# Second feed-forward layer with seven block products for eight in its up projections

## Chip, cores and metric

One core of one Trainium2 chip runs the whole kernel. The metric is the device time of one execution in microseconds. The kernel before takes 2902.94 us (median of 3 runs, 2902.27 to 2908.03).

## What is computed

The reference is a trunk of two layers on 1024 tokens of width 1024, with 16 meta tokens prepended: a neighbourhood attention, a grouped-query attention, and a feed-forward layer behind each. Only the second feed-forward layer is touched by the change:

```python
def rmsnorm(x, g):
    y = x32 * lax.rsqrt(jnp.mean(x32 * x32, axis=-1, keepdims=True) + RMS_EPS)
    return y.astype(x.dtype) * g

def swiglu(h, w1, w3, w2):
    return (jax.nn.silu(h @ w1) * (h @ w3)) @ w2

h = h + swiglu(rmsnorm(h, norm_ffn[i]), ffn_w1[i], ffn_w3[i], ffn_w2[i])
```

`h` has 1024 tokens here (the meta tokens are dropped after the attention of this layer), w1 and w3 are 1024 x 2816, w2 is 2816 x 1024, all float32.

## The kernel before

Everything is kept transposed: features on the 128 partitions, tokens along the free axis. The residual stream `h` is [128, 8, 1044], eight chunks of features. A float32 product is made of three passes in `fp32r`: each operand is split into a high part (rounded by writing it as `fp32r`) and a low part (what is left), and TensorE adds high x high, high x low and low x high. `uh` and `ul` hold the two parts of the input of the layer (`h` times its gain); the factor 1/rms of a token (`rstd`) is applied behind the product.

Weights come through two slots. SP loads a raw block into `wraw` (`fetch`, L384), GpSimd writes `wh` (L506, a multiplication by one) and `wl` (L509, the difference) and counts up `s_wrd`; TensorE multiplies the unit and counts up `s_un`, which frees the slot for GpSimd. A `unit` of the up projections (L695) is four feature chunks x three passes x two PSUM groups of 512 tokens, 24 matmuls with one weight block of 128 x 512; two units make a `dense`, one output block of 128 hidden columns.

`ffn(l)` works in rounds of 256 hidden columns, eleven of them (`FIT`). A round has four `dense` of the up projections (w1 and w3, for two output blocks b) in two sets of PSUM banks, and the down projections of the round before: eight units of 12 matmuls with weight blocks of 128 x 256. VectorE takes w1's product times rstd (L1571), ScalarE applies silu (L1212), VectorE multiplies by rstd (L1574) and by w3's product (L1577), ScalarE makes the high part of the gated row (L1214) and VectorE its low part (L1579). The down products are added to `h` by VectorE (L1559). The loops are written out per engine in the same order and are held together by counting semaphores: `s_wrd`, `s_un`, `s_df` (a PSUM group was read), `s_silu`, `s_sr`, `s_gh`, `s_gr`.

Ahead of the layer stands the output projection of the attention. Its adds to `h` feed squares (L1518 sums them), the parts `uh` and `ul` (L1197, L1522), and at its end `stat` (L729) and `rsqrt` with `refine` (L1528 to L1536), which leave `rstd`. Behind the layer stand the final norm and the stores. Steps of other stages which the rows below show are: the first projections (L1646 makes `ul`), the per-head norm of the attention (L1807, L1862), and its sum of probabilities on GpSimd (L648).

## Time and profile before

| | |
|---|---|
| median of the runs | 2902.94 us |
| profiled execution | 2904.71 us, span 2902.9 us |
| PE (matmul) busy | 2795.3 us, 96% |
| PEld (weight load) busy | 2293.9 us, 79% |
| VectorE (DVE) busy | 1264.5 us, 44% |
| ScalarE (ACT) busy | 663.5 us, 23% |
| GpSimd (POOL) busy | 1381.4 us, 48% |
| granted TensorE clock, mean | 0.986 |

The page gives for each engine the time in which it had an instruction in work, over the span of one execution. Matmuls overlap in the array, so their mean duration is longer than the distance between two starts. The chain that ended last goes back from the last instruction to what released it; a wait shows which engine's semaphore ended it. Over the whole span, 85% of that chain is PE.

### The profile page before, as it was taken

The page shows a single profiled execution, that of the slowest core. Times are in us where ns is not written, and L with a number is a line of the kernel's source. Part 1 is how long each engine was busy: PE and PEld are TensorE (multiplying, and loading weights), DVE is VectorE, ACT ScalarE, POOL GpSimd, SP SyncE. Part 2 cuts the span into 40 slices and gives each one's busy share as a digit, 9 for nine tenths or more (in the row PEclk, how much of TensorE's full clock was granted, in tenths as well). Part 3 has the DMA queues.
Part 4 walks back from the last instruction along what each step waited for, and adds up shares of the span by engine and source line. Part 5 has one row for each costly group of instructions (what it writes and reads, how often), then busy time and mean ns, then how long its engine had stood idle before and what let it go on. Part 6 is the DMA issues. An engine that isn't in the chain of part 4 may idle for free.

```text
span 2902.9 us, 39911 instructions
## 1 busy us (share of the span) xinstructions
PE 2795.3 (96%) x15103; PEld 2293.9 (79%) x15103; DVE 1264.5 (44%) x1644; ACT 663.5 (23%) x1132; POOL 1381.4 (48%) x1399
## 2 busy tenths in 40 slices
PE   6999999899999999999999999998799999999998
PEld 5888888699999999999776444443678888888886
DVE  4454444443322232222878766665352322322225
ACT  3333343311000000000332545543210000000003
POOL 3565555454444444444544745644354444444442
PEclk8999999999999999999999999999899999999999
DMA  8222121511111111111432000000311111111112
GB/s 201 58 72 61 58 66 47 199 44 46 44 47 46 44 46 46 46 47 46 136 70 55 8 15 1 15 15 16 145 44 44 51 51 47 47 47 47 45 45 84
DMA packets 227572, 166.17 MB, mean 57 GB/s; under 512 B 25000, under 2 KB 209744, under 8 KB 227296
## 3 DMA queue, kind: packets, MB, share of 16 engines
q1 hardware_dynamic: 215376, 135.69, 16.6%
q10 hardware_dynamic: 12048, 28.37, 2.7%
q8 instruction: 109, 1.79, 0.3%
q14 instruction: 39, 0.32, 0.0%
HBM read 133.19 MB, written 26.03 MB: 55 GB/s over the span
## 4 chain that ended last, share of the span: by engine, by line
PE 85%; DVE 8%; issue 3%; DMA 2%; ACT 1%; SPq 0%; ACTq 0%; POOL 0%; DVEq 0%; POOLq 0%
PE PS L695 60%; PE PS L822 8%; PE PS L1086 3%; DVE nmx L1900 3%; PE PS L873 2%; PE PS L1100 2%; PE PS L909 2%; PE PS L849 2%; DVE rcp L1929 2%; PE PS L1026 1%; DMA wraw<-in_a_w_qkv 1%; DVE accd L1916 1%; PE PS L887 1%; DVE ssq L1518 1%; PE PS L1044 1%
## 5 line engine op out<-in xcount | busy, mean ns | idle before, releaser
L506 POOL TENSOR_TENSOR wh<-wraw,ones 128x512 fp32r<-128x512 f32 (+1 forms) x456 | 426.7, 936 | 1174.1 <-PE PS L695 1010.2
L509 POOL TENSOR_TENSOR wl<-wraw,wh 128x512 fp32r<-128x512 f32 (+1 forms) x456 | 528.0, 1158 | 35.7
L695 PE MATMUL PS<-uh,wh 128*128 128x348 f32 (+1 forms) x1696 | 451.6, 361 | 18.9 <-DVE q L1670 7.5
L695 PE MATMUL PS<-uh,wl 128*128 128x348 f32 (+1 forms) x1696 | 445.8, 358 | 0.0
L695 PE MATMUL PS<-ul,wh 128*128 128x348 f32 (+1 forms) x1696 | 445.7, 358 | 0.0
L1559 DVE TENSOR_TENSOR h<-PS,h 128x1044 f32<-128x1044 f32 (+1 forms) x192 | 236.9, 1234 | 331.2 <-PE PS L695 316.6
L695 PEld LDWEIGHTS PS<-uh,wh 128*128 128x128 f32 x1696 | 302.1, 189 | 73.9 <-issue 22.5
L695 PEld LDWEIGHTS PS<-ul,wh 128*128 128x128 f32 x1696 | 304.3, 189 | 36.3
L695 PEld LDWEIGHTS PS<-uh,wl 128*128 128x128 f32 x1696 | 303.8, 189 | 36.2
L1212 ACT ACTIVATE at<-at 128x1044 f32<-128x1044 f32 (+1 forms) x44 | 47.1, 1070 | 862.9 <-DVE at L1571 862.9
L695 PE MATMUL PS<-yh,wh 128*128 128x348 f32 x1056 | 226.1, 323 | 5.3 <-DVE h L1559 2.9
L695 PE MATMUL PS<-yl,wh 128*128 128x348 f32 x1056 | 225.0, 321 | 0.0
L695 PE MATMUL PS<-yh,wl 128*128 128x348 f32 x1056 | 224.7, 321 | 0.0
L1571 DVE TENSOR_TENSOR at<-PS,rstd 128x1044 f32<-128x1044 f32 (+1 forms) x44 | 54.4, 1235 | 367.7 <-PE PS L695 367.7
L1900 DVE TENSOR_REDUCE nmx<-PS 128x1 fp32r<-128x1044 f32 x128 | 158.3, 1240 | 123.8 <-PE PS L1026 123.7
L1450 ACT ACTIVATE pf<-PS 128x512 f32<-128x512 f32 (+1 forms) x288 | 170.6, 595 | 180.1 <-PE PS L1086 178.8
L1577 DVE TENSOR_TENSOR at<-PS,at 128x1044 f32<-128x1044 f32 (+1 forms) x44 | 54.4, 1236 | 320.6 <-PE PS L695 320.5
L695 PEld LDWEIGHTS PS<-yh,wh 128*128 128x128 f32 x1056 | 177.8, 188 | 6.6 <-issue 6.4
L695 PEld LDWEIGHTS PS<-yl,wh 128*128 128x128 f32 x1056 | 178.7, 188 | 0.0
L695 PEld LDWEIGHTS PS<-yh,wl 128*128 128x128 f32 x1056 | 177.4, 188 | 0.0
L648 POOL TENSOR_TENSOR accp<-accp,pf 128x1024 f32<-128x1024 f32 x64 | 152.5, 2382 | 28.0 <-ACT pf L1450 25.0
L1100 PE MATMUL PS<-pf,vg 128*64 128x512 f32 x576 | 155.1, 617 | 0.0
(236 smaller groups left out, 3999.1 us busy)
## 6 DMA issues: line engine op xcount, KB each, us to landing
wraw<-in_ffn_w SPq DMA_DIRECT2D x176, 256.0 KB, 2.9
wraw<-in_ffn_w SPq DMA_DIRECT2D x176, 128.0 KB, 2.2
wraw<-in_a_w_qkv SPq DMA_DIRECT2D x48, 256.0 KB, 2.9
biasb<-bias_rows SPq DMA_DIRECT2D x128, 72.0 KB, 2.6
h<-h_spill ACTq DMA_DIRECT2D x16, 522.0 KB, 9.1
h_spill<-h SPq DMA_DIRECT2D x8, 522.0 KB, 8.8
h_spill<-h ACTq DMA_DIRECT2D x8, 522.0 KB, 3.3
xt<-in_x SPq DMA_DIRECT2D x8, 512.0 KB, 10.8
```

Source lines behind the costliest of these rows:

```text
L506: nc.gpsimd.tensor_tensor(wh[:, slot, 0:w], wraw[:, slot, 0:w], ones[:, 0:1].to_broadcast([P, w]), ALU.mult).then_inc(s_whi, 1)
L509: nc.gpsimd.tensor_tensor(wl[:, slot, 0:w], wraw[:, slot, 0:w], wh[:, slot, 0:w].bitcast(F32), ALU.subtract).then_inc(s_wrd, 1)
L648: nc.gpsimd.tensor_tensor(accp[:, :, :], accp[:, :, :], pf[:, (first + kt) % PB, :, :], ALU.add).then_inc(s_pacc, 1)
L695: mm = nc.tensor.matmul(PS[:, set_ + c, 0:cw], w, x[k][:, c * cw:(c + 1) * cw], start=(first and i == 0 and ti == 0), stop=(last and i == ...
L822: mm = nc.tensor.matmul(PS[:, D0 + bk, 0:CW], w, x[c][:, bk * CW:(bk + 1) * CW], start=(c == 0 and ti == 0), stop=(c == 7 and ti == 2), sk ...
L849: mm = nc.tensor.matmul(PS[:, 6 + hd, 0:SN], q, k[:, 5 * x:5 * x + WR + 1, K0[j]:K0[j] + WC], start=True, stop=True)
L873: mm = nc.tensor.transpose(PS[:, 3 + hd, P * c:P * c + P], pb[:, n % 4, a:a + P], ident[:, :])
L1086: mm = nc.tensor.matmul(PS[:, 6 + e, :], k[:, P * kt:P * kt + P], q[:, q0:q0 + QB], start=(i == 0), stop=(i == 1))
L1100: nc.tensor.matmul(PS[64 * e:64 * e + 64, OB[n % 2], :], vg[par][:, kt, :], pf[:, s % PB, e, :], start=(kt == 0), stop=(kt == KT - 1), ski ...
L1450: nc.scalar.activation(pf[q, s % PB, e, :], PS[q, 6 + e, :], ACT.Exp).then_inc(s_gex, 1)
L1559: nc.vector.tensor_tensor(hm, PS[:, set_:set_ + nb, 0:cw], hm, ALU.add).then_inc(s_df, 1)
L1900: nc.vector.tensor_reduce(nmx[:, i:i + 1], PS[:, set_:set_ + 3, 0:CW], AX.XY, ALU.max, negate=True).then_inc(s_mr, 1)
```

## The change

Rounds 2 to 11 of the layer compute their up projections by block products. With the 1024 features, the 256 hidden columns and the 1024 tokens each cut in two, a quad (w1 or w3 of one round) is a 2 x 2 block matrix product of eight blocks; it is made of seven products (Strassen's scheme in Winograd's form), each of 12 matmuls into one PSUM bank, with sums of weight blocks as one operand and sums of blocks of u as the other.

- GpSimd makes four sums of weight blocks for each quad (`sum_of`) and, as before, the high and low parts of each of the seven weight operands (`lo`), all 512 wide, in three slots (`wh3`, `wl3`) from six raw buffers (`rb`). The down projections take four weight loads of 512 a round in place of eight of 256.
- The four sums of u blocks are made once, in round 1: ScalarE writes `h` times gain in 16 copies of 512, VectorE makes four sums and four low parts of 2048, ScalarE four high parts (`block_hi`, `block_lo`). Round 1 itself stays as four `dense`, with its second output block first.
- ScalarE copies the first product of a quad (`snap`); VectorE adds the products up into blocks (`sums`, `gate_quad`, `gated_quad`) and then scales, gates and splits the rows.
- The order on TensorE is: w1's quad of the next round, the down projections of the last one, w3's quad of the next round. The last iteration has both quads and then two sets of down projections.
- Buffers are laid out anew (`ghs`, `ghl`, `tsh`, `tsl`, `bsum`, `upraw` and others).

```diff
+ROLES = [[(0, 1, 2, 3, 4), (1, 4, 2, 5, 3)], [(0, 1, 2, 3, 4), (5, 0, 2, 4, 1)]]
+QBANK = [(0, 1, 2, 7), (5, 3, 6, 4)]
...
+            def fetch_products():
...
+                sp.wait_ge(s_wrd, U_S)
+                sp.wait_ge(s_tl, 3)
+                first(U_S, 1)
+                down(DOWN[0][0], U_S, 0, 0)
+                with sp.Fori(0, ITS - 1) as i:
+                    rest(OPS * i + U_S, i)
+                    first(OPS * i + (U_S + OPS), i + 2)
+                    down(DOWN[0][0], OPS * i + (U_S + OPS), i + 1, 0)
...
-            fetch_ffn(1)
+            fetch_products()
...
+            def split_products():
+
+                def sum_of(dst, x, y, op, c):
+                    nc.gpsimd.tensor_tensor(rb[dst], rb[x], rb[y], op).then_inc(s_wsum, 1)
+                    po.wait_ge(s_wsum, c)
+
+                def lo(o, c, r, load=None):
+                    if load is not None:
+                        po.wait_ge(s_xr[r], load)
+                    po.wait_ge(s_un, U_S + c + (o - 3))
+                    nc.gpsimd.tensor_tensor(wh3[(o + 1) % 3], rb[r], ones[:, 0:1].to_broadcast([P, 512]),
+                                            ALU.mult).then_inc(s_xhi, 1)
+                    po.wait_ge(s_xhi, c + o)
+                    nc.gpsimd.tensor_tensor(wl3[(o + 1) % 3], rb[r], wh3[(o + 1) % 3].bitcast(F32),
+                                            ALU.subtract).then_inc(s_wrd, 1)
+
+                def quad(o, c, s, r, l22, l11, l21, l12):
+                    lo(o, c, r[A22], l22)
+                    lo(o + 1, c, r[A11], l11)
+                    po.wait_ge(s_xr[r[A21]], l21)
+                    sum_of(r[S3], r[A11], r[A21], ALU.subtract, s + 1)
+                    sum_of(r[A21], r[A21], r[A22], ALU.add, s + 2)
+                    sum_of(r[A11], r[A21], r[A11], ALU.subtract, s + 3)
+                    lo(o + 2, c, r[A11])
+                    lo(o + 3, c, r[A21])
+                    lo(o + 4, c, r[S3])
+                    lo(o + 5, c, r[A12], l12)
+                    po.wait_ge(s_wrd, U_S + c + o + 5)
+                    sum_of(r[A12], r[A12], r[A11], ALU.subtract, s + 4)
+                    lo(o + 6, c, r[A12])
...
-            split_ffn(1)
+            for q in range(4):
+                split_pair(U_FF[1] + 2 * q, U_FF[1] // 2 + q)
+            split_products()
...
+            def ffn_of_products():
+                ub, gb = U_FF[1], G_FF[1]
+
+                dense_of_new_u(ub, 3, gb - 2, 1, 5)
+                dense(ub + 2, D1, uhc, ulc, gb, 1)
+                dense(ub + 4, 5, uhc, ulc, gb + 1, 1)
+                pe.wait_ge(s_gm, 1)
+                dense(ub + 6, D1, uhc, ulc, gb + 1, 1)
+
+                def product(n, o, j, bank, first):
+                    pe.wait_ge(s_wrd, n + o)
+                    (xh, xl), a, b = operands[j], wh3[(o + 1) % 3], wl3[(o + 1) % 3]
+                    for k in range(4):
+                        for ti, (w, x) in enumerate(((a, xh), (a, xl), (b, xh))):
+                            mm = nc.tensor.matmul(PS[:, bank, :], w[:, P * k:P * k + P], x[:, k, :],
+                                                  start=(first and k == 0 and ti == 0),
+                                                  stop=(k == 3 and ti == 2), skip_group_check=True)
+                    mm.then_inc(s_un, 1)
+
+                def quad(n, o, t, banks_, adds=None):
+                    a, b, c, d = banks_
+                    if adds is not None:
+                        pe.wait_ge(s_ha, adds + 7)
+                    product(n, o, 0, d, True)
+                    if adds is not None:
+                        pe.wait_ge(s_ha, adds + 8)
+                    product(n, o + 1, 1, a, True)
+                    product(n, o + 2, 2, b, True)
+                    product(n, o + 3, 3, c, True)
+                    pe.wait_ge(s_u2, t)
+                    product(n, o + 4, 4, b, False)
+                    pe.wait_ge(s_snap, t)
+                    product(n, o + 5, 5, a, False)
+                    pe.wait_ge(s_c22, t)
+                    product(n, o + 6, 6, c, False)
...
+                pe.wait_ge(s_tl, 4)
+                with pe.Fori(0, ITS) as i:
+                    n = OPS * i + U_S
+                    pe.wait_ge(s_silu, 2 * i + (K1 + 2))
+                    quad(n, 1, 2 * i + 1, QBANK[0])
+                    pe.wait_ge(s_gr, 2 * i + (K1 + 2))
+                    for d in range(4):
+                        down(n, 8 + d, d, 0, (3, 5), loop_sets(i))
+                    quad(n, 12, 2 * i + 2, QBANK[1], 8 * i)
...
+                def sums(n, o, t, banks_):
+                    a, b, c, d = banks_
+                    dve.wait_ge(s_un, n + (o + 2))
+                    dve.wait_ge(s_snap, t)
+                    tt(u2, PS[:, b, :], s1, ALU.add, s_u2)
+                    dve.wait_ge(s_un, n + (o + 4))
+                    tt(u3[:, :], PS[:, b, :], s1, ALU.add, s_u3)
+                    dve.wait_ge(s_u3, t)
+
+                def gate_quad(n, o, t):
+                    a, b, c, d = QBANK[0]
+                    sums(n, o, t, QBANK[0])
+                    tt(at1[:, 1, right], PS[:, c, :], u3[:, :], ALU.add, s_c22)
+                    tt(at1[:, 1, left], u3[:, :], PS[:, d, :], ALU.subtract, s_c21)
+                    dve.wait_ge(s_c22, t)
+                    dve.wait_ge(s_c21, t)
+                    tt(at1[:, 1, :], at1[:, 1, :], r1, ALU.mult, s_ar)
+                    dve.wait_ge(s_un, n + (o + 5))
+                    tt(at1[:, 0, left], PS[:, a, :], r1[:, left], ALU.mult, s_c11)
+                    dve.wait_ge(s_un, n + (o + 6))
+                    dve.wait_ge(s_u2, t)
+                    tt(at1[:, 0, right], PS[:, c, :], u2, ALU.add, s_c12)
+                    dve.wait_ge(s_c12, t)
+                    tt(at1[:, 0, right], at1[:, 0, right], r1[:, right], ALU.mult, s_ar)
+
+                def gated_quad(n, o, t):
+                    a, b, c, d = QBANK[1]
+                    sums(n, o, t, QBANK[1])
+                    tt(c22[:, :], PS[:, c, :], u3[:, :], ALU.add, s_c22)
+                    tt(u3[:, :], u3[:, :], PS[:, d, :], ALU.subtract, s_c21)
+                    dve.wait_ge(s_c22, t)
+                    tt(at1[:, 1, right], at1[:, 1, right], c22[:, :], ALU.mult, s_b22)
+                    dve.wait_ge(s_c21, t)
+                    tt(at1[:, 1, left], at1[:, 1, left], u3[:, :], ALU.mult, s_gm)
+                    dve.wait_ge(s_un, n + (o + 5))
+                    tt(at1[:, 0, left], at1[:, 0, left], PS[:, a, :], ALU.mult, s_c11)
+                    dve.wait_ge(s_un, n + (o + 6))
+                    dve.wait_ge(s_u2, t)
+                    tt(u2, PS[:, c, :], u2, ALU.add, s_c12)
+                    dve.wait_ge(s_c12, t)
+                    tt(at1[:, 0, right], at1[:, 0, right], u2, ALU.mult, s_gm)
...
+                dve.wait_ge(s_un, ub + 2)
+                taken(1, 5)
+                dve.wait_ge(s_hgt, 2 * KC)
+                tt(b11, b12, b11, ALU.subtract, s_tt)
...
+                gate_row(1, 1)
+                dve.wait_ge(s_un, ub + 4)
+                gated(1, 1, D1)
+                for j, i in enumerate((0, 1, 3)):
+                    block_lo(i, j + 1)
+                dve.wait_ge(s_un, ub + 6)
+                taken(0, 5)
+                gate_row(0, 2)
+                block_lo(2, 4)
+                dve.wait_ge(s_un, ub + 8)
+                gated(0, 2, D1)
+                with dve.Fori(0, ITS) as i:
+                    n = OPS * i + U_S
+                    g_lo(1, 2 * i + 1, 0)
+                    g_lo(0, 2 * i + 2, 0)
+                    gate_quad(n, 1, 2 * i + 1)
+                    gate_row(1, 2 * i + 3)
+                    down(0, 3, *unit_sem(n, 8, 4 * i, 0), s_ha)
+                    gate_row(0, 2 * i + 4)
+                    for m in range(1, KC):
+                        down(m, 5 if m % 2 else 3, *unit_sem(n, 8, 4 * i, m), s_ha)
+                    dve.wait_ge(s_sr, 2 * i + (K1 + 4))
+                    gated_quad(n, 12, 2 * i + 2)
```

`OPS` is 18 and `ITS` 9 (rounds 2 to 10 in a loop, round 11 behind it). `tt` is VectorE's two-operand op, `r1` is `rstd`. `g_lo` makes the low part of a gated row, `gate_row` multiplies a row by `rstd`, both 1024 wide and from SBUF. `s_tl` counts the low parts of the u sums, `s_gm` gated rows, `s_ha` down products added to `h`.

## Rows read from the trace of the kernel before

**Rows 1.** The chain that ended last: start us, us, what.

```profile
2150.96 726.50 PE PS L695 x3144
```

**Rows 2.** Busy time of each engine in a stretch of the second feed-forward layer.

```profile
core 0: us, PE busy (x) PEld busy (x) DVE busy (x) ACT busy (x) POOL busy (x), PEclk, DMA share, GB/s
2200.00:2300.00 100.00, 100.00 (x435) 81.18 (x434) 27.03 (x22) 7.43 (x7) 43.20 (x44) 1.00 0.16 45
```

**Rows 3.** Groups by line and form, 2200 to 2800 us: count, busy us, mean ns, idle before.

```profile
L695 PEld LDWEIGHTS PS<-ul,wh 128*128 128x128 f32 x578 | 108.6, 188 | 25.1
```

**Rows 4.** GpSimd in order of time: start us, us, what, [idle before].

```profile
2467.28 1.04 POOL L506 TENSOR_TENSOR wh<-wraw,ones 128x512 fp32r<-128x512 f32 x1 [3.12 <-PE PS L695]
2468.40 1.30 POOL L509 TENSOR_TENSOR wl<-wraw,wh 128x512 fp32r<-128x512 f32 x1
```

**Rows 5.** All engines in order of time, 26 to 30 us.

```profile
27.09 2.15 POOL L509 TENSOR_TENSOR wl<-wraw,wh 128x512 fp32r<-128x512 f32 x1
29.20 2.04 POOL L506 TENSOR_TENSOR wh<-wraw,ones 128x512 fp32r<-128x512 f32 x1
...
29.49 0.92 PE L695 MATMUL PS<-uh,wh 128*128 128x348 f32 x2 [5.60 <-POOL wl L509]
```

**Rows 6.** Groups by line and form, whole run, as in rows 3.

```profile
L648 POOL TENSOR_TENSOR accp<-accp,pf 128x1024 f32<-128x1024 f32 x64 | 152.5, 2382 | 28.0 <-ACT pf L1450 25.0
...
L1862 DVE TENSOR_TENSOR qc<-qc,PS 128x512 f32<-128x512 f32 x4 | 2.7, 682 | 4.8 <-PE PS L971 4.8
```

**Rows 7.** All engines in order of time, 2400 to 2403 us.

```profile
2400.45 0.63 PE L695 MATMUL PS<-uh,wh 128*128 128x512 f32 x2
2400.65 1.23 DVE L1571 TENSOR_TENSOR at<-PS,rstd 128x1024 f32<-128x1024 f32 x1 [9.95 <-PE PS L695]
...
2400.76 1.04 POOL L506 TENSOR_TENSOR wh<-wraw,ones 128x512 fp32r<-128x512 f32 x1 [3.15 <-PE PS L695]
```

**Rows 8.** All engines in order of time, 2162 to 2170 us.

```profile
2163.91 2.20 DVE L1536 TENSOR_TENSOR rstd<-ssq,oraw 128x1024 f32<-128x1024 f32 x1
...
2166.14 1.23 DVE L1571 TENSOR_TENSOR at<-PS,rstd 128x1024 f32<-128x1024 f32 x1
...
2168.49 1.28 DVE L1574 TENSOR_TENSOR at<-at,rstd 128x1024 f32<-128x1024 f32 x1 [1.13 <-ACT at L1212]
...
2168.78 2.16 POOL L509 TENSOR_TENSOR wl<-wraw,wh 128x512 fp32r<-128x512 f32 x1
```

**Rows 9.** All engines in order of time, 1548 to 1552 us.

```profile
1548.90 1.09 DVE L1807 SCALAR_TENSOR_TENSOR ssq<-ssq,y_gq 96x512 f32<-96x512 f32 x1
...
1549.52 1.62 POOL L509 TENSOR_TENSOR wl<-wraw,wh 128x512 fp32r<-128x512 f32 x1
```

**Rows 10.** The page: a group of part 5, and part 6 (KB, us to landing).

```profile
L1450 ACT ACTIVATE pf<-PS 128x512 f32<-128x512 f32 (+1 forms) x288 | 170.6, 595 | 180.1 <-PE PS L1086 178.8
...
wraw<-in_ffn_w SPq DMA_DIRECT2D x176, 256.0 KB, 2.9
```

**Rows 11.** TensorE in order of time, behind two of its idle times.

```profile
573.13 0.74 PE L695 MATMUL PS<-uh,wh 128*128 128x348 f32 x3 [2.89 <-DVE h L1559]
...
574.24 1.07 PE L695 MATMUL PS<-uh,wl 128*128 128x348 f32 x3
...
577.64 0.64 PE L695 MATMUL PS<-uh,wh 128*128 128x348 f32 x3
...
2058.36 1.05 PE L695 MATMUL PS<-ol,wh 128*128 128x512 f32 x2
2059.22 1.05 PE L695 MATMUL PS<-oh,wl 128*128 128x512 f32 x2
```

**Rows 12.** Busy time and granted clock (PEclk) behind idle times, columns as in rows 2.

```profile
573.00:577.00 4.00, 3.87 (x16) 3.87 (x17) 3.24 (x4) 3.89 (x4) 0.68 (x1) 0.64 0.22 66
1107.00:1112.00 5.00, 3.61 (x23) 3.62 (x24) 1.16 (x1) 0.00 (x0) 2.28 (x2) 1.00 0.39 108
2057.00:2061.00 4.00, 3.65 (x9) 2.88 (x10) 0.21 (x1) 0.00 (x0) 0.00 (x0) 0.50 0.10 28
```

More of the change, by code:

```diff
@@ L91 @@
 ARR, EW = 23, 48
+OPS = 18
+SUMS = 8
+RAWS = 6
+A22, A11, A21, A12, S3 = range(5)
+ROLES = [[(0, 1, 2, 3, 4), (1, 4, 2, 5, 3)], [(0, 1, 2, 3, 4), (5, 0, 2, 4, 1)]]
+DOWN = [(5, 2, 4, 0), (3, 5, 2, 1)]
+TAIL = (0, 4, 3, 5)
+QBANK = [(0, 1, 2, 7), (5, 3, 6, 4)]
 def banks(ap, l=0):
@@ L290, in build @@
         G_WO, G_FF = [25, G_GQ], [34, G_GQ + 9]
-        G_ST = [0, 33, 166, G_FF[1] - 1, G_FF[1] + 132]
+        G_ST = [0, 33, 166, G_FF[1] - 1, G_FF[1] + 10]
+        U_S, ITS = U_FF[1] + 8, FIT - 2
+        U_L = U_S + OPS * ITS
+        K1 = 2 * FIT
         def kview(ap):
@@ L367, in build @@
         s_sum = sem("gqa_sums_done")
+        s_hgt = sem("u_of_ffn1_made")
+        s_tt = sem("u_block_sum_made")
+        s_tbh = sem("u_block_sum_hi_made")
+        s_tl = sem("u_block_sum_ready")
+        s_xr = [sem(f"up_raw{i}_loaded") for i in range(RAWS)]
+        s_wsum = sem("weight_block_sum_made")
+        s_xhi = sem("product_weight_hi_made")
+        s_snap = sem("first_product_copied")
+        s_u2 = sem("two_products_added")
+        s_u3 = sem("three_products_added")
+        s_c22 = sem("block22_made")
+        s_c21 = sem("block21_made")
+        s_c12 = sem("block12_made")
+        s_c11 = sem("block11_read")
+        s_b22 = sem("gated_block22_made")
+        s_ar = sem("gate_row_scaled")
+        s_gm = sem("gated_row_made")
+        s_dn = sem("down_unit_multiplied")
+        s_ha = sem("down_unit_added")
         block = es.enter_context(nc.Block())
@@ L717, in dense_of_new_u @@
                 xh, xl = chunks(u_hi[k]), chunks(u_lo[k])
-                unit(n, 0, D0, xh, xl, range(0, 4), True, False, l, KC * k)
+                unit(n, 0, set_, xh, xl, range(0, 4), True, False, l, KC * k)
                 if k:
@@ L722, in dense_of_new_u @@
                     spread_first()
-                unit(n + 1, 1, D0, xh, xl, range(4, 8), False, True, l, KC * k)
+                unit(n + 1, 1, set_, xh, xl, range(4, 8), False, True, l, KC * k)
             def spread(set_, w, x, l=0):
@@ L763, in down @@
                     pe.wait_ge(s_gr, k)
-                    xh, xl = [gh[l][par][:, b, :] for b in range(2)], [gl[l][par][:, b, :] for b in range(2)]
+                    xh, xl = [gh[par][:, b, :] for b in range(2)], [gl[par][:, b, :] for b in range(2)]
                     for m in range(KC):
@@ L1160, in _ @@
             proj_out(1)
-            ffn(1)
+            ffn_of_products()
             pe.wait_ge(s_ssq, 4)
-            pe.wait_ge(s_df, G_FF[1] + 132)
+            pe.wait_ge(s_df, G_FF[1] + 10)
             for i in range(8):
```

257 lines of the change are left out of this document (236 added, 21 removed).

## Prediction

> **What bounds the kernel now.** I read the chain of work that ended last first. From 2150.96 us it is one piece of 726.50 us, 3144 matmuls of `unit` (L695), and it ends 25 us before the span does [rows 1]. That piece is the second feed-forward layer but for its first 24 matmuls, so this layer is TensorE's: 0.2311 us a matmul of 512 columns (726.50 / 3144), 5.55 us for a unit of 24, 66.5 us for a round of 288. Busy time by stretch says the same: PE 100 of 100 us at full clock, GpSimd 43, VectorE 27 [rows 2]. TensorE is the only engine whose removed work is worth time here, and GpSimd has about half of each round free. The question is what GpSimd and VectorE do to each other once GpSimd is filled.
>
> **The change, part by part.** A round is the up projections of 256 hidden columns, in two quads A (w1) and B (w3), and the down projections D of the round before. Round 1 stays dense.
>
> *Matmuls.* A quad takes 7 products of 12 matmuls for 96: 12 fewer, twice a round, ten rounds: 240 x 0.2311 = **-55.5 us**. A product takes 2.77 us, a quad 19.4, D 22.2, a round 61.0. I keep 0.2311: each matmul has a weight load of its own already, 188 ns, beside a matmul of 231 [rows 3].
>
> *GpSimd's work.* A weight block costs 1.04 + 0.08 + 1.30 us [rows 4]; the next op starts 0.04 before the last ends (27.09 + 2.15 against 29.20) [rows 5]: 2.38 us a block. A sum of two blocks is a two-input op of 512: 1.30, as `wl`, and 0.08 for its own semaphore. The 1024-wide sum took 2382 ns [rows 6], so half of it, 1.19, is the lower bound; 1.40 is my upper. Down weights are now loaded 512 wide, four of 2.38 for eight smaller pairs. A quad is 7 x 2.38 + 4 x 1.38 = 22.2 us of GpSimd for 19.4 of TensorE; D is 9.5 for 22.2. The round's sum, 53.9, fits under 61.0, but the order is A, D, B, A, D, B: B and A follow each other, 44.4 us against 38.8, and with three weight slots GpSimd enters them only two blocks ahead. That is a local deficit whatever the averages say.
>
> *VectorE against GpSimd.* Here the trace speaks against the change. GpSimd's op of 1.04 is still 1.04 beside a VectorE op that reads PSUM (L1571, all of it overlapped) [rows 7]. Beside a VectorE op that reads two SBUF tensors, one waits for the other: `wl` at 2168.78 took 2.16 for 1.30, behind L1574; and the other way round L1536, started while a `wl` was in work, took 2.20 for 1.23 [rows 8]. So an op of 1024 costs GpSimd 2.16 - 1.30 = 0.86 us. For 512 wide: `wl` at 1549.52 took 1.62 beside L1807, that is 0.32 lost [rows 9]. The change adds such ops while GpSimd has no slack: `gate_quad` and `gated_quad` scale and multiply in SBUF (one of 1024 and four of 512 a round), and the two `g_lo` of 1024 now fall on the start of A. Ops on PSUM (`u2`, `u3`, blocks 22, 21, 12, the adds to `h`) cost GpSimd nothing. The Trainium skill ("SBUF — State Buffer", Who interferes with whom) states that a VectorE instruction with two SBUF inputs and a GpSimd one that reads SBUF exclude each other for the whole instruction. The row agrees with who is blocked, not quite with how long; by whole instructions (1.23 and 0.68) the stall below would be 1.8 us longer in each of nine rounds, 16 us more in all.
>
> *The stall in a round.* I follow GpSimd from the end of D. Blocks B1 and B2 are ready and B's three sums end 1.2 us later. Until A3 is ready come 8 blocks, 19.0, and 4 sums, 5.5; three VectorE ops of 512, 1.0; two `g_lo`, 1.7; waits for slots, 0.3 (a slot is free 0.31 after the next unit starts, 2400.76 against 2400.45 [rows 7]). Ready at 28.7 to 29.0. TensorE gets to A3 after nine products, 25.0. It restarts 0.25 after `wl` (27.09 + 2.15 to 29.49 [rows 5]): **4.25 us idle at A3**. From A4 on a product is longer than a block, so GpSimd keeps up but for the fourth sum and the `ar` op of 1024: 0.6 us at the first D. Nine times 4.85 = 43.7 us. The last round has no D between its quads: GpSimd needs 22.2 + 3 us of losses for B's 19.4, 5.5 idle, and some 1 in the downs: 6.5.
>
> *Start.* rstd is ready at 2166.1 and VectorE takes the first row then [rows 8]. New behind that on its queue: four block sums of 2048 (an estimate of 2 x 1.23 - 0.15 = 2.3 each), excluded by GpSimd's splits in turn (3.4 lost, and 0.9 for TensorE on a late split), before `gated(1)`, which now ends at 2183. The fourth dense of round 1 waits for it (`s_gm`), due at 2179: 4.0 late. Then three low parts, a row, silu, the last high part (which waits for unit 7) and low part: 2197, where TensorE is done at about 2194: 3.2. GpSimd's first blocks wait for loads that SP holds until `s_tl` 3: 1.15 at A1 and 5.2 at A3. Together 13.5.
>
> Other edits I cost at nothing. The loads: the closest one (A11 of B) is issued three units before its use, over 5 us, and a 256 KB load lands in 2.9 [rows 10]. PSUM reads: `u2`, `u3` and block 22 take 0.68 each [rows 6] and have a product of 2.77 to do it in. ScalarE's 16 copies of 512 for the block sums, 0.6 each [rows 10], are 9.6 us beside VectorE's rsqrt chain and over before it. The tail after the last add is unchanged.
>
> Sum so far: -55.5 + 43.7 + 6.5 + 13.5 = **+8.2 us**.
>
> *The clock.* What a stall does next decides the size. Behind 2.89 us without a matmul the granted clock was 0.64 in 573 to 577; behind the long wait that ends at 2057 it was 0.50 until 2061: the lower of the two levels, 1.2 GHz for 2.4, at which matmuls of 512 start 0.43 apart [rows 11, 12]. The 5 us from 1107, with 1.4 idle, kept 1.00 [rows 12]. There will be eleven stalls of over 4 us. A low stretch of about 3.4 us (574.2 to 577.6 in rows 11) costs 8 x (0.43 - 0.231) = 1.6; 0.5 of that is taken from the stall at D; 1.1 x 11 = **+12 us**. Bounds: nothing, and twice that stretch (the long wait had at least 4 us), 30.
>
> Total +20 us. The profiled execution took 2904.71, with a span of 2902.9, 1.8 above the median of the runs; the difference applies to either: **2923 us**.
>
> **The rivals.**
> 1. *The exclusion costs nothing* (VectorE's ops fall into gaps of GpSimd). The stall at A3 is then 28.9 - 2.7 + 0.25 - 25.0 = 1.5; that at D goes, the start costs 6 and the last quad 3: 22 in all, no stall long enough for the clock. -55.5 + 22 = -33: **2869**. For it: averages leave room. Against it: GpSimd has no gaps between B and A, and rows 8 and 9 show the loss whenever two such ops meet. It decides from the point where stalls in a round, clock included, are under 3.9 us (55.5 less 20 for start and end, over nine).
> 2. *The port costs as above, but the clock stays up*: +8: **2911**. For it: a gap of 1.4 us did nothing; against it both longer ones.
> 3. *The clock stays low twice as long*: +8 + 30: **2941**.
> 4. *Half-way*: sums of 1.19 (4 x 0.11) and half of the meetings avoided (1.4) take 1.8 off each stall at A3, which is then 2.4 and mostly too short for the clock: 8.2 - 9 x 1.8 - 4 at start and end, -12: **2891**.
> That the change does not do what it says, TensorE paying per product what it saves, I give 2 in 100: nothing in rows 3 hints at it.
>
> **How the numbers follow.** Forecast 0.45; rival 1 0.15; 2 0.17 (half of its spread inside 0.2%); 3 0.12; 4 0.09; the last 0.02. This measurement can tell about 0.2%, 5.8 us, from no change. Faster: 0.15 + 0.09 = 0.24. Same: 0.12. Slower: 0.64. The forecast's own range is 2910 to 2942; the range for 8 in 10 reaches down towards rival 1 and over rival 3: 2878 to 2946.
>
> **What would show it.** In the profile after: about 240 fewer matmuls; a round near 66.9 us against 66.5; PE at some 91% in this layer, with ten idle times of over 4 us at the third product of A, ended by GpSimd's `wl`; GpSimd near 90%, its ops of 1.04 and 1.30 at 1.4 to 2.2 where `g_lo` or `ar` meets them; VectorE's `g_lo` at 2.0 to 2.3 for 1.23; a granted clock of 0.95 to 0.97 there. It is wrong if GpSimd's mean op stays at 1.04 and 1.30, if idle at A3 is under 3 us, or if another engine ends the wait (VectorE through `s_c22` or `s_ha`, a load).

## The result, and the profile after

The changed kernel takes 2926.01 us (median of 4 runs, 2923.73 to 2930.06) against 2904.65 for the kernel before (4 runs, 2902.27 to 2908.03): ratio 1.0074, 95% interval 1.0056 to 1.0092. It is slower by 21 us, where 2923.0 was forecast. The profiled execution has a span of 2921.9 us at a mean granted clock of 0.975 (before 2902.9 and 0.986).

In the lines of after, L920 issues the matmuls of the block products, L954 those of the down projections, L852 the dense ones; GpSimd makes sums at L646, high parts at L653, low parts at L656; nearly all of VectorE's work is L1917, so there one goes by tiles (`gls` is written by `g_lo`).

The page, part 1 (busy us, share of the span, instructions): 14863 matmuls where there were 15103, so 240 fewer; GpSimd has 281 us more, VectorE 142.

```profile
PE 2763.1 (95%) x14863; PEld 2266.0 (78%) x14863; DVE 1406.7 (48%) x1782; ACT 692.4 (24%) x1172; POOL 1661.9 (57%) x1511
```

Busy time by stretch, columns as in [rows 2], which is the same stretch of before:

```profile
2200.00:2300.00 100.00, 91.30 (x379) 73.87 (x378) 44.56 (x42) 8.16 (x9) 85.33 (x66) 0.95 0.18 53
2200.00:2800.00 600.00, 561.00 (x2354) 455.34 (x2353) 275.51 (x256) 46.88 (x52) 510.22 (x394) 0.96 0.16 47
2273.00:2277.00 4.00, 4.00 (x10) 3.14 (x11) 0.00 (x0) 0.00 (x0) 3.84 (x4) 0.50 0.30 96
```

TensorE is busy 91.3 of 100 us where it was busy all of them, and GpSimd 85.3 where it had 43. The third row lies right behind a wait: clock 0.50, the lower of its two levels (1.2 GHz for 2.4).

The waits of TensorE between 2150 and 2900 us (us in total, times, longest), for its matmuls:

```profile
PE PS L920 <- POOL wl L656: 48.4, 13, 4.4
PE PS L852 <- DVE at L1917: 3.0, 1, 3.0
PE PS L852 <- POOL wl L620: 0.6, 1, 0.6
```

All but 4 us of it is GpSimd's `wl`, ahead of a block product. In order of time on TensorE (start, us, what, [idle before]), with the last matmul ahead of a wait, the first ones behind it, the step back to full speed, and two later waits:

```profile
2268.27 0.39 PE L920 MATMUL PS<-uh,wl 128*128 128x512 f32 x1
2272.93 0.80 PE L920 MATMUL PS<-tsh,wh 128*128 128x512 f32 x1 [4.27 <-POOL wl L656]
2273.53 0.63 PE L920 MATMUL PS<-tsl,wh 128*128 128x512 f32 x1
2273.95 0.63 PE L920 MATMUL PS<-tsh,wl 128*128 128x512 f32 x1
...
2278.22 0.63 PE L920 MATMUL PS<-tsh,wh 128*128 128x512 f32 x1
2278.65 0.44 PE L920 MATMUL PS<-tsl,wh 128*128 128x512 f32 x1
...
2340.60 0.80 PE L920 MATMUL PS<-tsh,wh 128*128 128x512 f32 x1 [4.28 <-POOL wl L656]
...
2836.94 0.80 PE L920 MATMUL PS<-tsh,wh 128*128 128x512 f32 x1 [4.32 <-POOL wl L656]
```

A3, the third product of A, is the `tsh` product behind the one that reads `uh` (A2; A1 reads `tsh` too). Round 2 waits 4.43 us there, as part of the start; then come nine such waits, one a round, of 4.20 to 4.28, and one of 4.32 at the third product of the last B: eleven. Behind each, matmuls of 512 start 0.43 apart, then 0.23. From one restart at A3 to the next it is 67.67, 66.35, 67.25, 67.68, 66.40, 67.24, 68.67 and 67.47 us: 67.3 in the mean, where a round took 66.5 before. The rounds differ by the length of the slow stretch at their start: 3.1 us of it go with 66.4, 4.9 with 67.2 and 5.7 to 6.0 with 67.5 to 67.7 (the one of 68.67, with 6.1, also has TensorE wait for VectorE's adds in D).

What GpSimd and VectorE do in front of the wait that ends at 2272.93:

```profile
2259.59 1.79 POOL L656 TENSOR_TENSOR wl<-wraw,wh 128x512 fp32r<-128x512 f32 x1
2261.34 1.49 POOL L653 TENSOR_TENSOR wh<-wraw,ones 128x512 fp32r<-128x512 f32 x1
2262.91 1.29 POOL L656 TENSOR_TENSOR wl<-wraw,wh 128x512 fp32r<-128x512 f32 x1
2263.92 0.83 DVE L1917 TENSOR_TENSOR at<-at,ssq 128x512 f32<-128x512 f32 x1
2264.16 1.75 POOL L646 TENSOR_TENSOR upraw<-wraw,upraw 128x512 f32<-128x512 f32 x1
2264.67 4.55 DVE L1917 TENSOR_TENSOR gls<-at,ghs 128x1024 fp32r<-128x1024 f32 x2
2265.98 2.16 POOL L646 TENSOR_TENSOR upraw<-upraw,wraw 128x512 f32<-128x512 f32 x1
2268.22 2.12 POOL L646 TENSOR_TENSOR wraw<-upraw,wraw 128x512 f32<-128x512 f32 x1
2270.50 1.04 POOL L653 TENSOR_TENSOR wh<-wraw,ones 128x512 fp32r<-128x512 f32 x1 [0.16 <-POOL wraw L646]
2271.62 1.26 POOL L656 TENSOR_TENSOR wl<-wraw,wh 128x512 fp32r<-128x512 f32 x1
```

Block 2 of A is done at 2264.2; the three sums stand between it and block 3, and all are stretched: 1.75, 2.16 and 2.12 for 1.29. The first meets the last product of 512 of `gated_quad` (`at<-at,ssq`), the other two meet the `gls`, which cost them 0.87 + 0.83 = 1.70. Two products of 512 just before had met block 1's low part (1.79 for 1.30) and block 2's high part (1.49 for 1.04). Two `gls` take 4.55 for 2 x 1.23. In the groups of 2200 to 2800 us the plain sum is 1291 ns, the third sum of A, which meets `gls`, 2030, and `gls` 2315:

```profile
L646 POOL TENSOR_TENSOR upraw<-upraw 128x512 f32<-128x512 f32 x27 | 34.9, 1291 | 1.4
L646 POOL TENSOR_TENSOR wraw<-upraw,wraw 128x512 f32<-128x512 f32 x9 | 18.3, 2030 | 0.7
L1917 DVE TENSOR_TENSOR gls<-at,ghs 128x1024 fp32r<-128x1024 f32 x16 | 36.4, 2315 | 0.0
```

### The profile page after: what moved, and what is told of

Read it like the earlier page. It is cut to its first block, busy times and chain, and to the rows that moved or that the text cites. A ratio compares the mean times of both kernels' runs of the same rounds, so it can differ in the third digit from the quotient of the medians.

```text
span 2921.9 us, 39631 instructions
## 1 busy us (share of the span) xinstructions
PE 2763.1 (95%) x14863; PEld 2266.0 (78%) x14863; DVE 1406.7 (48%) x1782; ACT 692.4 (24%) x1172; POOL 1661.9 (57%) x1511
## 4 chain that ended last, share of the span: by engine, by line
PE 62%; POOL 14%; DVE 10%; issue 9%; DMA 2%; ACT 1%; SPq 0%; POOLq 0%; ACTq 0%; DVEq 0%
PE PS L852 34%; PE PS L1070 8%; POOL wh L653 6%; POOL wl L656 3%; POOL upraw L646 3%; PE PS L1334 3%; DVE nmx L2335 3%; PE PS L1348 2%; PE PS L1121 2%; PE PS L954 2%; PE PS L1157 2%; PE PS L1097 2%; DVE rcp L2364 2%; PE PS L920 2%; PE PS L1274 1%
## 5 line engine op out<-in xcount | busy, mean ns | idle before, releaser
L617 POOL TENSOR_TENSOR wh<-wraw,ones 128x512 fp32r<-128x512 f32 (+1 forms) x288 | 289.5, 1005 | 800.0 <-PE PS L852 644.6
L620 POOL TENSOR_TENSOR wl<-wraw,wh 128x512 fp32r<-128x512 f32 (+1 forms) x288 | 361.0, 1253 | 22.6
L852 PE MATMUL PS<-uh,wh 128*128 128x348 f32 (+1 forms) x1056 | 253.0, 343 | 19.2 <-DVE q L2105 8.0
L852 PE MATMUL PS<-uh,wl 128*128 128x348 f32 (+1 forms) x1056 | 246.2, 337 | 0.0
L852 PE MATMUL PS<-ul,wh 128*128 128x348 f32 (+1 forms) x1056 | 245.9, 336 | 0.0
L852 PE MATMUL PS<-yh,wh 128*128 128x348 f32 x1056 | 226.1, 323 | 5.0 <-DVE h L1866 2.9
L852 PE MATMUL PS<-yl,wh 128*128 128x348 f32 x1056 | 225.0, 321 | 0.0
L852 PE MATMUL PS<-yh,wl 128*128 128x348 f32 x1056 | 224.7, 321 | 0.0
L852 PEld LDWEIGHTS PS<-uh,wh 128*128 128x128 f32 x1056 | 183.5, 191 | 46.3 <-issue 21.5
L852 PEld LDWEIGHTS PS<-ul,wh 128*128 128x128 f32 x1056 | 184.4, 190 | 8.8
L852 PEld LDWEIGHTS PS<-uh,wl 128*128 128x128 f32 x1056 | 183.2, 190 | 8.6
L656 POOL TENSOR_TENSOR wl<-upraw,wh 128x512 fp32r<-128x512 f32 x131 | 177.9, 1358 | 10.3
L852 PEld LDWEIGHTS PS<-yh,wh 128*128 128x128 f32 x1056 | 177.8, 188 | 6.3 <-issue 6.1
L852 PEld LDWEIGHTS PS<-yl,wh 128*128 128x128 f32 x1056 | 178.7, 188 | 0.0
L852 PEld LDWEIGHTS PS<-yh,wl 128*128 128x128 f32 x1056 | 177.4, 188 | 0.0
L653 POOL TENSOR_TENSOR wh<-upraw,ones 128x512 fp32r<-128x512 f32 x131 | 149.8, 1143 | 46.8 <-PE PS L954 36.4
L1917 DVE TENSOR_TENSOR h<-PS,h 128x1024 f32<-128x1024 f32 x88 | 107.4, 1221 | 92.1 <-PE PS L954 92.1
```

The lines of the kernel that those rows point to most:

```text
L617: nc.gpsimd.tensor_tensor(wh[:, slot, 0:w], wraw[:, slot, 0:w], ones[:, 0:1].to_broadcast([P, w]), ALU.mult).then_inc(s_whi, 1)
L620: nc.gpsimd.tensor_tensor(wl[:, slot, 0:w], wraw[:, slot, 0:w], wh[:, slot, 0:w].bitcast(F32), ALU.subtract).then_inc(s_wrd, 1)
L653: nc.gpsimd.tensor_tensor(wh3[(o + 1) % 3], rb[r], ones[:, 0:1].to_broadcast([P, 512]), ALU.mult).then_inc(s_xhi, 1)
L656: nc.gpsimd.tensor_tensor(wl3[(o + 1) % 3], rb[r], wh3[(o + 1) % 3].bitcast(F32), ALU.subtract).then_inc(s_wrd, 1)
L852: mm = nc.tensor.matmul(PS[:, set_ + c, 0:cw], w, x[k][:, c * cw:(c + 1) * cw], start=(first and i == 0 and ti == 0), stop=(last and i == ...
L1917: nc.vector.tensor_tensor(out_, x, y, op).then_inc(sem_, 1)
```

## The experiments

Three questions: does the clock cost what was forecast; is the wait at A3 one of GpSimd's load, of its meetings with VectorE, or of the order of its work; and is there a version that beats both kernels? All are edits of the changed kernel. "Wait" is TensorE's idle time of 0.3 us or more in a round.

**1. The clock.** Sixteen matmuls that nobody reads, ahead of every A3 and of B3 of the last round, the eleven places:

```diff
+                    for f in range(16 if adds is None else 0):
+                        nc.tensor.matmul(PS[:, b, :], uh[:, f % 4, 0:P], uh[:, f % 4, 0:512],
+                                         start=True, stop=True)
```

> The changed kernel with 16 extra matmuls of 512 columns (3.7 us) ahead of the third product of A in every round, and of B in the last: TensorE works through its stall instead of waiting. Their sums are thrown away. Theory (the low clock behind each stall costs time): TensorE's wait there falls from 4.27 us to about 0.6 with GpSimd still the one that ends it, the clock stays at the upper level, a round falls from 67.3 us to about 65.9, the whole by 13 to 17 us, to about 2911. Rival (the low stretches cost nothing, GpSimd's pace hides them): rounds and time unchanged, 2926. Rival (the wait is not idle time that can be filled): 11 x 3.7 us slower, 2967.

Measured: 2912.08 us, ratio to the kernel before 1.0020 (1.0011 to 1.0030). The wait at A3 is 0.59, a round 65.7, and the clock 1.00 in 2200 to 2800:

```profile
2200.00:2800.00 600.00, 591.40 (x2555) 477.24 (x2556) 293.06 (x264) 50.83 (x57) 531.78 (x403) 1.00 0.16 47
```

The data come no sooner (16 x 0.231 + 0.59 = 4.29), yet 14 us are gone. So the low clock behind the eleven waits costs 14 us, net of what comes back elsewhere (a wait of 0.31 at the first D of each round, which the change hides behind its slow matmuls): this is the answer to rival 2, which priced the same kernel without that loss at 2911.

**2. The two `g_lo` alone.** Their operand comes from PSUM in place of SBUF:

```diff
-                    tt(g2l[g][:, b, :], at1[:, b, :], g2h[g][:, b, :].bitcast(F32), ALU.subtract, s_gr)
+                    tt(banks(g2l[g][:, b, :], 1), PS[:, 3:5, :], banks(g2h[g][:, b, :], 1).bitcast(F32), ALU.subtract, s_gr)
```

> The changed kernel with one operand of g_lo in the loop (two VectorE ops of 1024 a round) read from PSUM banks 3 and 4 instead of the gated row in SBUF: the same widths and the same order, but only one SBUF operand. Left out: the right low part of the gated rows. Theory (VectorE ops with two SBUF operands hold GpSimd up by 0.86 us each): g_lo falls from 2.3 us to 1.23, the GpSimd sums beside it from 1.75 and 2.15 to 1.30, the wait at A3 from 4.27 to about 2.5, a round to between 65.6 (clock still falls) and 64.2; the whole to 2898 to 2912. Rival (GpSimd's backlog is its own work alone): the wait stays at 4.27 and the time at 2926.

Measured: 2902.75, ratio 0.9996 (0.9986 to 1.0006); the wait 2.60, 1.67 shorter, a round 64.8. Two `g_lo` of 1024 take 1.67 us of GpSimd, where the prediction had 1.7. Beside `gls` with one operand in PSUM the second sum takes its plain 1.29; the first stays at 1.76, since what it meets is the product of 512:

```profile
2456.36 1.76 POOL L646 TENSOR_TENSOR upraw<-wraw,upraw 128x512 f32<-128x512 f32 x1
2456.87 2.43 DVE L1917 TENSOR_TENSOR gls<-PS,ghs 128x1024 fp32r<-128x1024 f32 x2
2458.19 1.29 POOL L646 TENSOR_TENSOR upraw<-upraw,wraw 128x512 f32<-128x512 f32 x1
```

The clock still falls behind all nine waits at A3, for 2.7 to 3.5 us. A round is 2.5 us shorter: 1.67 of waiting, the rest beside shorter slow stretches.

**3. All of VectorE's ops with two SBUF operands** in the rounds, cut to 16 columns or fed from PSUM:

```diff
-                    tt(at1[:, b, :], at1[:, b, :], r1, ALU.mult, s_sr)
+                    tt(at1[:, b, 0:16], at1[:, b, 0:16], r1[:, 0:16], ALU.mult, s_sr)
...
-                    tt(at1[:, 1, left], at1[:, 1, left], u3[:, :], ALU.mult, s_gm)
+                    tt(at1[:, 1, 0:16], at1[:, 1, 0:16], u3[:, 0:16], ALU.mult, s_gm)
```

> As the last one, and the other VectorE ops of the loop with two SBUF operands (the scalings ar and gate_row, the gate products of 512) cut to 16 columns. Left out: those products and scalings beyond 16 columns, and the right low part. Theory: the wait at A3 falls to 1.5 us, what GpSimd's own 28.9 - 2.7 us leave; round 62.7; clock near 1.00 in the rounds; the whole near 2880. If it stays above 3 us, the backlog is not from the shared port; if it is 0, sums and blocks are cheaper than I have them.

Measured: 2870.57, one run; the wait 1.17, a round 61.8, no low clock in it. GpSimd's ops from B3 to A3 all take 1.04 and 1.28 to 1.30. So rival 1 had the kernel without exclusion about right (1.5 us at A3, 2869 in all; its start was too cheap, 6 us for waits of 9.2, and its A3 too dear), and exclusion makes 3.1 of the 4.27 us at A3; 1.2 is load and order.

**4. GpSimd with little to do**: sums, and two of three low parts, 16 columns wide, and the fifth block made from A12 in place of a sum.

```diff
-                    nc.gpsimd.tensor_tensor(rb[dst], rb[x], rb[y], op).then_inc(s_wsum, 1)
+                    nc.gpsimd.tensor_tensor(rb[dst][:, 0:16], rb[x][:, 0:16], rb[y][:, 0:16], op).then_inc(s_wsum, 1)
```

> The changed kernel with GpSimd's load cut down: all sums and two of three low parts only 16 columns wide (left out: the rest of them, and the third sum block). It shows what TensorE alone does with 240 matmuls fewer. Theory: no wait of TensorE for GpSimd inside the rounds, round 61.0 us, 55.5 us less than before in matmuls, 5 to 9 us of waits at the start: the whole 2854 to 2862. If a product were dearer than 2.77 us, or VectorE's sums a limit of their own, a round would be over 62 us.

Measured: 2853.67; no wait in any round, TensorE busy 600.00 of 600 us. This is one run. The 240 matmuls are thus worth 51 us with the start paid, and in the rounds no other engine holds TensorE up.

**5. High parts by ScalarE.** Is it load? ScalarE, busy 8 of 100 us, makes the high parts of blocks 1, 2, 5 and 6 of A and 5 and 6 of B:

```diff
+                def w_hi(n, o, r, sem_, need):
+                    act.wait_ge(sem_, need)
+                    act.wait_ge(s_un, n + (o - 3))
+                    nc.scalar.activation(wh3[(o + 1) % 3], rb[r], ACT.Copy).then_inc(s_ahi, 1)
...
```

> The changed kernel with the high parts of six of the 18 weight blocks of a round made by ScalarE (blocks 1, 2, 5 and 6 of A, 5 and 6 of B), everything else as it is. Nothing is left out. Theory (GpSimd's backlog from B3 to A3 is the cost): four of the eight high parts in that stretch leave GpSimd, 4 x 1.12 = 4.5 us and with them some meetings with VectorE; the wait at A3 goes to under 0.5, a round to 61.0 to 61.7 us, the clock stays up; the whole falls by 9 x 5.9 and 3 at the end, to about 2868, faster than the kernel before (2904). Rival (another limit stands right behind GpSimd, VectorE's sums or ScalarE's queue, which now has 6 more ops of 0.6): a round over 64, the whole over 2893, with VectorE or ACT ending TensorE's waits.

Measured: 2905.76, ratio 1.0002 (0.9991 to 1.0013): 20 us better than the change, but 38 short of what was expected. The wait is 2.31, and the clock low behind eight of nine. GpSimd and VectorE in order of time, and TensorE's restart:

```profile
2522.01 1.29 POOL L667 TENSOR_TENSOR wl<-wraw,wh 128x512 fp32r<-128x512 f32 x1 [1.49 <-ACT wh L1534]
2523.27 1.29 POOL L649 TENSOR_TENSOR upraw<-wraw,upraw 128x512 f32<-128x512 f32 x1
2524.64 1.29 POOL L649 TENSOR_TENSOR upraw<-upraw,wraw 128x512 f32<-128x512 f32 x1
2524.82 1.66 DVE L1947 TENSOR_TENSOR at<-at,ssq 128x512 f32<-128x512 f32 x1
2526.01 1.63 POOL L649 TENSOR_TENSOR wraw<-upraw,wraw 128x512 f32<-128x512 f32 x1
2526.40 4.30 DVE L1947 TENSOR_TENSOR gls<-at,ghs 128x1024 fp32r<-128x1024 f32 x2
2527.79 1.82 POOL L664 TENSOR_TENSOR wh<-wraw,ones 128x512 fp32r<-128x512 f32 x1 [0.16 <-POOL wraw L649]
2529.70 2.12 POOL L667 TENSOR_TENSOR wl<-wraw,wh 128x512 fp32r<-128x512 f32 x1
...
2531.87 0.80 PE L933 MATMUL PS<-tsh,wh 128*128 128x512 f32 x1 [2.31 <-POOL wl L667]
```

GpSimd is no longer late when it comes to block 2: it idles 1.49 us for it. Block 2 cannot begin before its slot is free, and from there to A3 runs a fixed chain: high part 0.63 by ScalarE, low part 1.29, three sums, high and low part of block 3. That is 9 us but for the `gls`, against three products, 8.3, on TensorE; the `gls` add 0.78 + 0.83 = 1.61 on block 3. (The third sum's 0.34 belongs to the product of 512, `at<-at,ssq`, and stays in experiment 10.) Taking load off did not shorten this chain.

**6. The order.** One sum ahead of block 1, one between blocks 1 and 2, one behind:

```diff
-                    lo(o, c, r[A22], l22)
-                    lo(o + 1, c, r[A11], l11)
+                    po.wait_ge(s_xr[r[A22]], l22)
+                    po.wait_ge(s_xr[r[A11]], l11)
                     po.wait_ge(s_xr[r[A21]], l21)
                     sum_of(r[S3], r[A11], r[A21], ALU.subtract, s + 1)
+                    lo(o, c, r[A22], l22)
                     sum_of(r[A21], r[A21], r[A22], ALU.add, s + 2)
+                    lo(o + 1, c, r[A11], l11)
                     sum_of(r[A11], r[A21], r[A11], ALU.subtract, s + 3)
```

> The changed kernel with GpSimd's sums in another order: the first ahead of the quad's first block, the second between its first two blocks, the third behind the second block, instead of all three there. Nothing is left out. Theory (GpSimd has too much work between B3 and A3): the same work must be done, only B's first two sums move into the idle time of D, so that B3 starts 0.9 us earlier; the wait at A3 falls from 4.27 to 3.2 to 3.5, a round by 1 us, the whole to about 2916. Rival (it is the row of three sums, which TensorE outlives with two blocks in hand, not the total): the wait goes under 1.5 us and the time under 2890.

Measured: 2911.08, ratio 1.0022 (1.0011 to 1.0032). The waits of a round are now 1.87 at A2, 1.73 at A3 and 0.32 at the first D, 3.9 in sum against 4.27. Hardly anything was gained in idle time; the low clock behind most of them went. In the two rounds that still have it the wait at A3 is under 0.3 and the round is as long as the others, 65.4 us: GpSimd sets the pace there, and a slower TensorE waits less. The first quad of all waits 8.06 us at A1 instead of 4.43 at A3, since its first sum needs three loads.

**7. Both, 5 and 6.**

> The last two together: six high parts of a round by ScalarE, and the sums spread out. Nothing is left out. In the run with ScalarE alone the wait at A3 was 2.3 us while GpSimd itself waited for slots and for ScalarE, so with less work the limit has become the way from the release of a slot over high part, low part and three sums to A3: 0.3 + 0.6 + 1.3 + 4.1 + 2.4 = 8.7 us and two g_lo, against three products, 8.3. Theory: with two of the three sums ahead of it that way is 6 us and the wait at A3 is under 0.5; a round is 61.0 to 61.8 us, the clock stays up in the rounds, the whole about 2868. Rival (GpSimd is still too slow in the total, or ScalarE is late): the wait stays over 1.5 and the time over 2890.

Measured: 2891.22, ratio 0.9954 (0.9938 to 0.9971). Faster than before, and 23 us over what was expected. The wait at A3 is 1.90, where under 0.5 was named. Again GpSimd and VectorE in order of time:

```profile
2520.23 1.74 POOL L649 TENSOR_TENSOR wraw<-upraw,wraw 128x512 f32<-128x512 f32 x1
2520.74 4.29 DVE L1949 TENSOR_TENSOR gls<-at,ghs 128x1024 fp32r<-128x1024 f32 x2
2522.12 1.82 POOL L664 TENSOR_TENSOR wh<-wraw,ones 128x512 fp32r<-128x512 f32 x1 [0.16 <-POOL wraw L649]
2524.03 2.13 POOL L667 TENSOR_TENSOR wl<-wraw,wh 128x512 fp32r<-128x512 f32 x1
```

Both `gls` still fall on block 3: 0.78 + 0.83 = 1.61 us, most of the wait. The last sum's 0.45 is the product of 512 again; it is still there in experiment 9 (1.75), where the `gls` are gone from block 3 and the wait is 0.29.

**8. The `g_lo` moved**, behind `u2` of the next quad A, three products later:

```diff
                     tt(u2, PS[:, b, :], s1, ALU.add, s_u2)
+                    if mid is not None:
+                        g_lo(1, mid + 1, 0)
+                        g_lo(0, mid + 2, 0)
...
-                    g_lo(1, 2 * i + 1, 0)
-                    g_lo(0, 2 * i + 2, 0)
```

> The changed kernel with VectorE's two g_lo of a round moved from the start of A to behind u2, that is behind A's third product; the down products that read them come four products later still. Nothing is left out. Theory (it matters where VectorE's two-operand ops fall): the wait at A3 falls from 4.27 by 2 x 0.86 to 2.5, as with the operand from PSUM, but the two now hold up GpSimd's fourth to sixth blocks of A, where a product is 0.39 us longer than a block, so that some 0.5 to 1.3 us come back ahead of A5 to A7; round 66.0 to 66.8 with the clock still falling behind the wait, the whole 2906 to 2918. Rival (a meeting costs the same wherever it falls, since GpSimd is full over the whole round): time unchanged within 4 us, 2926.

Measured: 2912.77, ratio 1.0022 (1.0007 to 1.0038). The wait at A3 is 2.58, shorter by 1.69. But with GpSimd short of time all through the quad the cost comes back at the block that the ops meet now: in the two rounds whose clock stays up, two further waits of 0.44 and 1.75 follow, and these rounds are 66.1 us long, the others 65.7.

**9. All three**: 5 and 8, and two sums between blocks 1 and 2 (which spares the first quad the wait for three loads).

> ScalarE's six high parts, two of the three sums ahead of the quad's second block, and the g_lo behind u2. Nothing is left out. In the run with the first two, A3's wait was 1.9 us, and three of GpSimd's ops on the way to it were stretched by 0.44 to 0.86 each, by g_lo above all. Theory: without them the way fits, the wait at A3 is under 0.3 and what comes back in A4 to A7 under 0.6, since two of those blocks are low parts alone; a round 61.0 to 61.9, clock up, the start 2 us better than there; the whole 2862 to 2872, 33 to 43 us faster than the kernel before. Rival (GpSimd's total is the limit): at least half of the 1.9 comes back later in A and the whole stays over 2880.

Measured: 2870.75 (2868.61 to 2872.65), ratio 0.9881 (0.9864 to 0.9897). No wait of over 0.3 us in the rounds; what is left is the start (0.58, 2.96, 3.63, 0.52) and 4.11 in the last B.

**10. Which of the three was needed?** 5 and 8 with the sums where the change put them.

> ScalarE makes the high parts of blocks 1, 2, 5 and 6 of A and 5 and 6 of B, and VectorE's g_lo come behind u2; the sums stay behind block 2. With the high parts at ScalarE alone the wait at A3 was 2.31 us, because the three sums stand between block 2 and block 3 and the g_lo meet them. If those meetings are what was left, moving the g_lo takes 1.7 us off: 0.6 us at A3, a round of 61.0 + 0.6 with no low clock, about 2875 with a last quad as after the change (2868 to 2882). If the g_lo only move their cost to the block that they meet later, the wait stays near 2 us: 2895 to 2905.

Measured: 2873.8 (2 runs), ratio 0.9895 (0.9866 to 0.9923); against experiment 9 the intervals overlap, so the sums ahead are not shown to add anything. The wait is 0.66 to 0.69, no low clock in the rounds. The same chain as in experiment 5:

```profile
2506.87 1.30 POOL L667 TENSOR_TENSOR wl<-wraw,wh 128x512 fp32r<-128x512 f32 x1 [1.49 <-ACT wh L1534]
2508.13 1.30 POOL L649 TENSOR_TENSOR upraw<-wraw,upraw 128x512 f32<-128x512 f32 x1
2509.50 1.30 POOL L649 TENSOR_TENSOR upraw<-upraw,wraw 128x512 f32<-128x512 f32 x1
2510.88 1.62 POOL L649 TENSOR_TENSOR wraw<-upraw,wraw 128x512 f32<-128x512 f32 x1
2512.66 1.04 POOL L664 TENSOR_TENSOR wh<-wraw,ones 128x512 fp32r<-128x512 f32 x1 [0.16 <-POOL wraw L649]
2513.78 1.28 POOL L667 TENSOR_TENSOR wl<-wraw,wh 128x512 fp32r<-128x512 f32 x1
...
2515.11 0.50 PE L933 MATMUL PS<-tsh,wh 128*128 128x512 f32 x1 [0.69 <-POOL wl L667]
```

Block 3 takes 1.04 and 1.28, not 1.82 and 2.12, and the wait is shorter by 1.62. Against experiment 5 this is one edit, the place of two ops of VectorE: 32 us, of which 9 x 1.63 = 14.7 is waiting at A3. The rest, 17, was not taken apart; most of it stands beside the clock that no longer falls in the rounds (eight slow stretches of 3.1 to 3.4 us there, 1.5 to 1.7 each).

**11. And without ScalarE?** The two sums early and the `g_lo` late, all high parts at GpSimd.

> Two of the three sums ahead of block 2 and VectorE's g_lo behind u2; GpSimd keeps all high parts. GpSimd's work for B and A then stays 44 us against 38.8 of TensorE, so waits stay, cut by the 1.7 us of the g_lo if these are hidden: 2.6 us a round in two or three pieces, each too short for the low clock as far as the rounds with the sums early alone showed: 2926 - 14 - 9 x 1.7 = 2897 (2890 to 2908). If order were all that matters, as the kernel with all three changes would allow too, it should be as fast as that one: 2871.

Measured: 2915.95, ratio 1.0039 (1.0023 to 1.0055): a miss by 19 us. TensorE's waits in a round:

```profile
2467.77 0.50 PE L921 MATMUL PS<-uh,wh 128*128 128x512 f32 x1 [1.41 <-POOL wl L656]
2471.55 0.50 PE L921 MATMUL PS<-tsh,wh 128*128 128x512 f32 x1 [0.76 <-POOL wl L656]
2480.49 0.50 PE L921 MATMUL PS<-uh,wh 128*128 128x512 f32 x1 [0.43 <-POOL wl L656]
2485.27 0.50 PE L921 MATMUL PS<-uh,wh 128*128 128x512 f32 x1 [1.75 <-POOL wl L656]
```

1.41 + 0.76 + 0.43 + 1.75 = 4.35: the 4.27 of the change, cut into four. I had taken the meetings with `gls` as gone; they only fall on later blocks, and as long as GpSimd is the slower engine over B and A every microsecond lost there reaches TensorE. The 10 us gained on the change stand beside a clock that stays up (1.00 in 2200 to 2800, against 0.96); that it is the cause rests on experiment 1.

Experiments 5, 8 and 10 together say what the wait is. Over B and A GpSimd has more work than TensorE, so neither order nor place takes the waits away until load is taken off (5); once it is, what counts is the chain from slot 2 to A3, and the `g_lo` in it (10).

## Why the prediction was right

*The mechanism.* TensorE was the bound, 240 matmuls went, and GpSimd became the bound over the stretch B, A of each round, not in the average of the round (85 of 100 us busy, where the text said near 90). The signs named came: waits at A3 ended by `wl`, `g_lo` at 2.3, and a granted clock of 0.96 in the rounds (0.95 to 0.97 named). The layer, from the row sum at its start to its last matmul, became longer by 21.4 us: 749.9 (2146.98 to 2896.87) for 728.5 (2148.97 to 2877.44). Forecast was 20.

Term by term, us:

| term | forecast | in the runs |
|---|---|---|
| 240 matmuls | -55.5 | -55.5 by the same step |
| nine waits at A3 | +38.3 | +38.4 (4.20 to 4.28 each) |
| first D, nine times | +5.4 | +0.3, one of 0.31, for VectorE's `h` (in experiment 1, where the clock stays up, GpSimd causes one in each round) |
| last quad and downs | +6.5 | +4.3 |
| start | +13.5 | +9.0 (0.56, 2.96, 1.06, 4.43) |
| clock | +12 | +24.9 |
| sum | +20.2 | +21.4 |

The first five are read as idle times. The clock's term is the rest, and it can be held against experiment 1: there the layer takes 733.9 us, of it 15.9 idle, 40.7 for eleven times sixteen matmuls (by 0.2311 each) and 672.7 for the others (728.2 - 55.5), which leaves 4.6. Of that, 2.9 is the slow stretch behind the wait for the gated row at the start, which the changed kernel has too (0.67 in the 7 us from 2182). So about 20 of the 24.9 stand behind the eleven waits, 1.8 each; read off the starts, as what the matmuls of the slow stretches took beyond 0.2311, it is 24, or 2.2 each, so the term is good to some 4 us. Of these 14 to 16 would be won by a clock that stays up.

*The wait at A3*, 4.25 forecast and 4.27 measured, is right in its parts too: 3.1 by the meetings (the text had 2.7) and 1.2 without (1.5). Of the 3.1, 1.67 are the `g_lo` (1.7), and 1.4 the three products of 512 (0.49, 0.45 and 0.46 in the lines above, where the prediction took 0.32 each from [rows 9]). The rows of before that carried it were [rows 8] and [rows 9]: 0.86 and 0.32 us lost by meetings that occurred a few times in a kernel where GpSimd had slack. The rule of the Trainium skill ("SBUF — State Buffer", Who interferes with whom) that the port pair which such ops share is an exclusive lock holds here as to who waits. That one waits for the other's whole instruction (words that the Trainium skill has beside VectorE's 2-port modes) does not: two `g_lo` cost 1.67 us and not 2 x 1.23. Its exemption of ops with at most one SBUF operand is what experiment 2 shows (1.29 beside `gls<-PS`).

*The clock.* Here the step that failed is the length of a low stretch, and the total held because other terms were too high by as much (4.5, 2.2 and 5.1 against 12.9): that they cancelled is luck. A stretch was taken as 3.4 us; behind six of the nine waits at A3 it was 4.9 to 6.1 (from 2272.93 the matmuls are slow until 2278.65) and 3.1 behind three, 4.7 in the mean, between the forecast and rival 3, which had twice 3.4. Rival 3's price of 30 us was too high, and it left the stalls at D and the long start beside it. The clock and D together were forecast at 17.4 and measured 25.2.

*Mis-sized terms.* The start was 4.5 too high: the 3.2 for the low parts of the block sums did not occur, the wait for the gated row was 3.0, not 4.0, and A3 of round 2 waited 4.4, not 5.2. The low parts were in time for A1: GpSimd had nothing to do from 2181.4 to 2191.2 (it waited for a load), and three of them took 7.55, 2.5 each. The last quad was 2.2 too high. Two of the prediction's sums are also off by a little: the parts of the start give 14.4 with the 0.9 for the late split (measured 0.56), not 13.5, and 22.2 + 3 against 19.4 leaves 5.8 in the last quad, not 5.5. Sums cost 1.29 + 0.08, which is the 1.38 chosen and rules out the 1.19 of rival 4.

*What fell* was my theory after the result: that load alone sets the wait. Experiment 5 was expected to remove it and left 2.31; experiment 7 left 1.90. In experiment 5 the step that failed is the count of GpSimd's work against TensorE's over a stretch, without the chain of dependent ops between a slot's release and the product that needs it. In experiment 7 the chain was counted, at 6 us, but not what VectorE's ops add to it: the `gls` alone added 1.61. In experiment 11 it was the reverse: the chain was shortened and load decided.
